# Experts of 96 slots in column tiles, with raw f32 weights, in place of 128 slots with split weights

## The reference

```python
g_idx = jnp.argmax(g_logits, axis=-1)
e_top, e_idx = lax.top_k(e_logits, TOP_K)              # TOP_K = 2 of 4 in that group
gates = jnp.sum(jax.nn.one_hot(ids, N_EXPERTS, dtype=f32) * e_w[..., None], axis=-2)
for e in range(N_EXPERTS):                              # 16 experts
    y = (jax.nn.silu(h @ w_gate[e]) * (h @ w_up[e])) @ w_down[e]   # 1024 -> 256 -> 1024
    out = out + gates[..., e:e + 1] * y.astype(f32)
```

## Time and profile before

| | |
|---|---|
| median of three runs | 513.7 us (513.49 to 515.2) |
| profiled execution, span from first to last instruction | 514.0 us |
| first gate/up product of the experts starts | 317.27 us |
| last down product ends | 480.59 us |
| TensorE busy | 464.2 us, 90% of the span |
| TensorE weight loads | 380.7 us, 74% |
| VectorE busy | 361.1 us, 70% |
| ScalarE busy | 257.9 us, 50% |
| GpSimd (POOL) busy | 104.8 us, 20% |
| DMA | 93.17 MB, mean 181 GB/s |

### The profile page before, as it was taken

The page is one execution under the profiler, slowest core; times in us unless marked ns, Lnnn a source line. Parts: engine busy times, 40 slices in busy tenths (PEclk is TensorE's granted clock), DMA queues, the critical chain, the costliest instruction groups (busy, mean ns, idle before and its releaser), DMA issues.

```text
span 514.0 us, 7284 instructions
## 1 busy us (share of the span) xinstructions
PE 464.2 (90%) x2541; PEld 380.7 (74%) x2541; DVE 361.1 (70%) x682; ACT 257.9 (50%) x484; POOL 104.8 (20%) x167
## 2 busy tenths in 40 slices
PE   6999899999999999999999988899999999999300
PEld 6879799878897777777787778787787778688100
DVE  4877515585676455776653769899998998998176
ACT  6663720643266436342231154588578678685021
POOL 5248001010100000000010032021323133132244
PEclk9999999999999999999989968899999999999855
DMA  8804404004006610510101598999999999921294
GB/s 303 201 11 166 172 0 160 5 1 164 1 2 178 157 62 0 177 49 1 42 1 62 162 342 311 421 383 405 357 344 396 379 365 376 355 92 46 80 341 179
DMA packets 32958, 93.17 MB, mean 181 GB/s; under 512 B 10104, under 2 KB 13312, under 8 KB 26784
## 3 DMA queue, kind: packets, MB, share of 16 engines
q1 hardware_dynamic: 27728, 82.81, 44.7%
q0 software_dynamic: 5200, 9.97, 5.2%
HBM read 87.85 MB, written 13.89 MB: 198 GB/s over the span
## 4 chain that ended last, share of the span: by engine, by line
PE 69%; DVE 15%; DMA 6%; ACT 4%; issue 3%; POOL 1%; SPq 1%; POOLq 0%; DVEq 0%; ACTq 0%
PE ps L1786 8%; PE ps L1788 7%; PE ps L1787 7%; PE ps L2140 4%; PE ps L2142 4%; PE ps L2141 4%; DVE gu_lo L1636 4%; PE ps L1998 3%; PE ps L1999 3%; PE ps L2000 3%; DMA xg<-h_rows,now_tok 2%; DMA pair<-y_pairs 2%; PE ps L2120 2%; PE ps L2023 2%; PE ps L2114 1%
## 5 line engine op out<-in xcount | busy, mean ns | idle before, releaser
L1636 DVE TENSOR_TENSOR gu_lo<-we_gu,gu_hi 128x1024 fp32r<-128x1024 f32 x64 | 74.4, 1220 | 0.8
L1016 ACT ACTIVATE gu_hi<-we_gu 128x1024 fp32r<-128x1024 f32 x64 | 63.3, 1057 | 0.0
L2140 PE MATMUL ps<-gu_hi,xT_hi 128*128 128x512 f32 x128 | 52.8, 412 | 3.3 <-DVE xT_lo L1630 3.2
L2142 PE MATMUL ps<-gu_hi,xT_lo 128*128 128x512 f32 x128 | 50.9, 398 | 0.0
L2141 PE MATMUL ps<-gu_lo,xT_hi 128*128 128x512 f32 x128 | 50.5, 394 | 0.0
L1786 PE MATMUL ps<-hT_hi,w_hi 128*128 128x288 f32 x160 | 48.6, 304 | 1.6 <-DVE w_lo_q L1129 0.8
L1786 PE MATMUL ps<-w_hi,hT_hi 128*128 128x512 f32 x96 | 38.9, 405 | 0.0
L1787 PE MATMUL ps<-w_lo,hT_hi 128*128 128x512 f32 x96 | 37.5, 390 | 0.0
L1786 PEld LDWEIGHTS ps<-hT_hi,w_hi 128*128 128x128 f32 x160 | 30.1, 188 | 5.0 <-issue 2.6
L2140 PEld LDWEIGHTS ps<-gu_hi,xT_hi 128*128 128x128 f32 x128 | 24.6, 192 | 9.6 <-issue 2.5
L826 ACT ACTIVATE w_hi<-ring,g_col 128x512 fp32r<-128x512 f32 (+1 forms) x48 | 28.8, 679 | 0.3 <-DMA ring<-in_w_in 0.3
(11 more groups left out here) (404 smaller groups left out, 1220.7 us busy)
## 6 DMA issues: line engine op xcount, KB each, us to landing
we_gu<-in_w_gate SPq DMA_DIRECT2D x16, 1024.0 KB, 8.3
we_gu<-in_w_up SPq DMA_DIRECT2D x16, 1024.0 KB, 12.9
we_d<-in_w_down SPq DMA_DIRECT2D x16, 1024.0 KB, 12.3
ring<-in_w_in SPq DMA_DIRECT2D x4, 2048.0 KB, 7.7
pair<-y_pairs SPq DMA_DIRECT2D x8, 512.0 KB, 7.8
ring<-in_w_in SPq DMA_DIRECT2D x3, 1024.0 KB, 8.3
x_first<-in_x_p SPq DMA_DIRECT2D x4, 512.0 KB, 9.9
x<-in_x_p SPq DMA_DIRECT2D x4, 512.0 KB, 3.9
```

The lines of the kernel that those rows point to most:

```text
L1016: act.activation(gu_hi[slot % 2][:, :, 2 * q:2 * q + 2, :], we_gu[slot][:, :, 2 * q:2 * q + 2, :], ACT.Copy).then_inc(gu_hi_done, 1)
L1636: dve.tensor_tensor(gu_lo[slot][:, :, 2 * q:2 * q + 2, :], we_gu[slot][:, :, 2 * q:2 * q + 2, :], gu_hi[slot % 2][:, :, 2 * q:2 * q + 2, : ...
L2140: pe.matmul(bank(0), xT_hi[:, c, :], gu_h[:, :, c, :], start=c == 0, stop=False)
L2142: last = pe.matmul(bank(0), xT_lo[:, c, :], gu_h[:, :, c, :], start=False, stop=c == KC - 1)
```

## The change

An expert gets 96 slots (`CAP`). Four experts fill 384 columns, which are three blocks of 128 (`PER`). The columns of a block are cut into column tiles of one width, each of one expert: block 0 is 96 columns of expert 0 and 32 of expert 1 (four tiles of 32), block 1 has 64 of expert 1 and 64 of expert 2 (two tiles of 64), block 2 has 32 of expert 2 and 96 of expert 3 (four tiles of 32). All products of the experts are plain f32 on raw weights; the splits and their buffers are gone.

```diff
+CAP = 96
+QUAD = 32
+PER = UNROLL * CAP // P
+MAX_OVER = (PAIRS - NE) // CAP
+AHEAD = 3
+def runs_of(b):
+    out = []
+    for q in range(P // QUAD):
+        u = (P * b + QUAD * q) // CAP
+        if out and out[-1][2] == u:
+            out[-1][1] += QUAD
+        else:
+            out.append([QUAD * q, QUAD, u])
+    return out
+def tiles_of(b):
+    runs = runs_of(b)
+    width = QUAD if any(n % (2 * QUAD) for _, n, _ in runs) else 2 * QUAD
+    return [(at + d, width, u) for at, n, u in runs for d in range(0, n, width)]
+PIECES = [(0, 0, 0, 96, 0), (0, 1, 0, 32, 96),
+          (1, 1, 32, 32, 0), (1, 1, 64, 32, 32), (1, 2, 0, 64, 64),
+          (2, 2, 64, 32, 0), (2, 3, 0, 32, 32), (2, 3, 32, 32, 64), (2, 3, 64, 32, 96)]
...
 # TensorE
-                    gu_h, gu_l = gu_hi[slot % 2], gu_lo[slot]
                     for c in range(KC):
-                        pe.matmul(bank(0), xT_hi[:, c, :], gu_h[:, :, c, :], start=c == 0, stop=False)
-                        pe.matmul(bank(0), xT_hi[:, c, :], gu_l[:, :, c, :], start=False, stop=False)
-                        last = pe.matmul(bank(0), xT_lo[:, c, :], gu_h[:, :, c, :], start=False, stop=c == KC - 1)
+                        for at_col, n, u in tiles_of(b):
+                            cols = slice(at_col, at_col + n)
+                            last = pe.matmul(ps[cols, 0, :], xT[:, c, cols], we_gu[u][:, :, c, :],
+                                             start=c == 0, stop=c == KC - 1)
                     last.then_inc(gu_ready, 1)
+                    pe.wait_ge(gathered[following], 16 * (i + (b + 1) // PER + 1))
+                    turn_half(following, 0, x_turned_a)
+                    turn_half(following, 1, x_turned_b)
+                    if b:
+                        down(i, b - 1)
+                    elif i is not first:
+                        down(i - 1, PER - 1)
+                    if i is first and b == PER - 1:
+                        over_slots()
                     pe.wait_ge(hh_ready, s + 1)
 # in down(i, b)
                 for half in range(2):
                     for f in range(2):
+                        for at_col, n, u in tiles_of(b):
+                            cols = slice(at_col, at_col + n)
+                            last = pe.matmul(ps[cols, 4 + 2 * (b % 2) + half, :], hhT[:, f, cols],
+                                             we_d[u][:, f, 512 * half:512 * half + 512], start=f == 0, stop=f == 1)
 # ScalarE and VectorE, per block, in this order
+                    act.activation(sg[:, :], ps[:, 0, 0:FE], ACT.Silu).then_inc(silu_ready, 1)
+                    take_x(s + 1)          # half of xT each
+                    take_y(i, b - 1)       # or (i - 1, PER - 1)
...
+                    dve.tensor_tensor(hh[:, :], sg[:, :], ps[:, 0, FE:2 * FE], ALU.mult).then_inc(hh_ready, 1)
+                    take_x(s + 1)
+                    take_y(i, b - 1)
+                    dve.tensor_copy(hhT[:, :, :], ps[:, 3, 0:2 * P].rearrange("p (c t) -> p c t", c=2)).then_inc(hhT_ready, 1)
 # VectorE, the table: nine pieces for each of the two tables
+            for b in range(PER):
+                fill(table_tok, 5, range(NE, 2 * NE), 0, b).then_inc(table_ready, 1)
 # SP
             expert(1, 1, 0, 2)
+            sp.wait_ge(out_ready, 2 * NT)
+            expert(2, 2, 0, 2)
             store_h2(NT - 1)
-            expert(0, 0, 2, 3)
-            expert(1, 1, 2, 3)
+            expert(3, 3, 0, 2)
...
             sp.wait_ge(gathered[0], 16)
+            for u in range(UNROLL):
+                expert(u, u, 2, 3)
+            with sp.Fori(1, TURNS) as i:
+                sp.wait_ge(gu_ready, PER * i - PER + 1)
+                expert(0, UNROLL * i, 0, 2)
+                sp.wait_ge(gu_ready, PER * i - PER + 2)
+                expert(1, UNROLL * i + 1, 0, 2)
+                sp.wait_ge(y_ready, PER * i - PER + 1)
+                expert(0, UNROLL * i, 2, 3)
+                sp.wait_ge(gu_ready, PER * i)
+                expert(2, UNROLL * i + 2, 0, 2)
+                expert(3, UNROLL * i + 3, 0, 2)
+                sp.wait_ge(y_ready, PER * i - PER + 2)
+                expert(1, UNROLL * i + 1, 2, 3)
+                sp.wait_ge(y_ready, PER * i)
+                expert(2, UNROLL * i + 2, 2, 3)
+                expert(3, UNROLL * i + 3, 2, 3)
 # POOL
-            for s in range(AHEAD):
+            for s in range(PER):
+                pool.wait_ge(table_ready, s + 1)
                 gather(s, table_tok[:, s:s + 1])
```

More of the change, by code:

```diff
@@ L601, in _ @@
                         e = sp.value_load(steer[0:1, bass.ds(UNROLL * i + slot + 1, 1)], min_val=0, max_val=NE - 1)
-                        expert(slot, e)
-            for par in range(2):
-                sp.wait_ge(stored[par], 8 * UNROLL * turns + 16)
+                        expert(slot, e, 0, 2)
+                        sp.wait_ge(y_ready, PER * i + PER * TURNS - (1 if slot < 2 else 0))
+                        expert(slot, e, 2, 3)
+            for b in range(PER):
+                sp.wait_ge(stored[b], 16 * more + 16 * TURNS + 16)
@@ L683, in _ @@
             pool.sem_inc(bias_ready, 1)
[L684 to L685 removed]
+            for out, n, first, step in ((iota16, NE, 0, 1), (iota8, OVER_UNITS, 0, 1),
+                                        (iota_p, P, 0, 1), (limits, TERMS, CAP, CAP)):
                 chain(pool.iota(out[:, :], pattern=[[step, n]], base=first, channel_multiplier=0,
@@ L746, in _ @@
                 gather(s, table_tok[:, s:s + 1])
-            pool.wait_ge(table_ready, 2)
+            pool.wait_ge(table_ready, PER + 1)
             pool.wait_ge(x_turned_b, 1)
[L749 to L760, removed]
@@ L784, in _, with scatter_later @@
-            with pool.Fori(1, turns) as i:
-                gather_next(i, 1)
-                for k in range(2, UNROLL + 1):
-                    gather_next(i, k)
-                    scatter_later(i, k - 2)
-                scatter_later(i, UNROLL - 1)
+                gather(b, now_tok[:, b, :])
+            def scatter_later(i, b):
+                s = PER * i + b - 2
+                was = (b - 2) % PER
+                pool.wait_ge(stored[was], 16 * i + (16 if b == 2 else 0))
+                pool.tensor_copy(now_pair[:, was, :], table[:, bass.ds(s, 1)]).then_inc(col_copied, 1)
+                pool.wait_ge(col_copied, 2 * PER * i - 2 * PER + 2 * b + 2)
+                pool.wait_ge(y_act, s + 1)
+                pool.wait_ge(y_dve, s + 1)
+                pool.sem_inc(dma_cleared, 1)
+                scatter(was, now_pair[:, was, :])
@@ new lines, in _ @@
+            with pool.Fori(1, more + TURNS) as i:
+                for b in range(PER):
+                    gather_next(i, b)
+                    scatter_later(i, b)
+            for b in range(PER - 2, PER):
+                s = PER * more + PER * TURNS - PER + b
+                pool.wait_ge(stored[b], 16 * more + 16 * TURNS)
+                pool.tensor_copy(now_pair[:, b, :], table[:, bass.ds(s, 1)]).then_inc(col_copied, 1)
+                pool.wait_ge(col_copied, 2 * PER * more + 2 * PER * TURNS - 2 * PER + b - PER + 3)
+                pool.wait_ge(y_act, s + 1)
+                pool.wait_ge(y_dve, s + 1)
+                pool.sem_inc(dma_cleared, 1)
+                scatter(b, now_pair[:, b, :])
@@ L1087, in _ @@
+            with act.Fori(1, more + TURNS) as i:
                 group_of_blocks(i)
+            take_y(more + TURNS - 1, PER - 1)
             for t in range(NT):
@@ L1697, in group_of_blocks @@
-                take_y(i, UNROLL - 1)
-            def down_low(i, slot):
-                for f in range(2):
-                    dve.wait_ge(d_hi_done, 2 * SHORT * i + 2 * slot + f + 1)
-                    dve.tensor_tensor(we_d_lo[slot][:, f, :], we_d[slot][:, f, :], we_d_hi[:, f, :].bitcast(F32),
-                                      ALU.subtract).then_inc(d_lo_done, 1)
+                    take_x(s + 1)
+                    if i is first and b == 0:
+                        weights()
+                    if b:
+                        take_y(i, b - 1)
+                    elif i is not first:
+                        take_y(i - 1, PER - 1)
```

391 lines of the change are left out of this document (135 added, 256 removed).

## The result

The changed kernel takes 506.24 us (median of four runs, 506.04 to 507.54), the kernel before beside it 513.6. The ratio is 0.9855, with a 95% interval of 0.9827 to 0.9884: 7.4 us faster. The forecast was 496.5, 17.2 us faster. The direction was right, and so was the mechanism of the steady blocks; the step at the start (the first chain of products at full pace) failed, and the size with it. Ratios are of fast executions alone, so that one execution of the kernel before, of 1592.6 us beside e5 to e8, does not count.

The account below looks back on a forecast made before the run. TensorE was taken to bound the kernel. First product at 318.3, first chain, ten blocks of 11.86 us, waits and tail put the last product at 463.4; 33.4 more gave span 496.8, time 496.5 us, range 489 to 503.

Parts of the forecast that it names:

- the mechanism of the steady blocks: Expert blocks on TensorE: tiles run beside each other, three blocks taking 35.6 us against 39.6 to 40.2 before.
- the first chain of products at full pace: First block's gate/up products on TensorE: eight steps at 0.86 us, 6.88 us.
- the changes of shape: Borders between column tiles and full-width work on TensorE: 0.5 us a block, bounds 0 and 1.0.
- the way from span to time: Final conversion: predicted span 496.8 us, measured median 0.3 us below the profiled span, so 496.5.
- A step of four tiles costs one plain product: Gate/up steps on TensorE: all tiles run beside each other, 0.86 us a step; bounds up to 3.44.
- A block, 11.86 us: Steady block on TensorE: gate/up 6.88, down 3.44, other work 1.04, shape changes 0.5 us.
- Weights hide: Expert weight loads: some 9 us in hand holds the whole lag, counted as nothing; other bound 8.4 us.
- The case of DMA in the lead: Rival: weight transfers set the pace, three groups at 38.4 us, +8.4 us, 505; chance 0.09.
- The start: Ahead of the experts: gather 2.5 us slower, first product moves from 317.27 to 318.3, between 316.4 and 321.
- The case of a falling clock: Rival: a long stretch of plain products could be granted 1.2 GHz, time above 620 us; chance 0.03.
- The end: After the last gate/up: 9.5 us to the end of the last product, then an unchanged 33.4 us.

Follow-up runs that it names:

- e5: Changed kernel with gate/up requests of experts 2 and 3 both behind the last store of h2; 508.33 us, ratio 0.9836.
- e8: Changed kernel with gate/up products issued tile by tile in place of step by step; 651.88 us in a single execution.
- e1: Changed kernel with one full-width tile per step, so part of the result is not computed; 500.81 us, ratio 0.9753.
- e6: Changed kernel with all tiles 32 wide, hh transposed next to x, hhT in three buffers and copied ahead of y; 503.29 us, ratio 0.9753.
- e11: e6 plus last h2 store ahead of expert 2's request, expert 3's gate/up request after the first gather, 36 idle products for 30; 498.66 us, ratio 0.969.
- e4: Changed kernel with expert 3's gate and up requested after the first gather landed, in place of before it; 504.81 us, ratio 0.9812.
- e9: Changed kernel with last h2 store ahead of expert 2's request, expert 3's gate/up request after the first gather, 36 idle products; 500.59 us, ratio 0.9755.
- e3: Changed kernel with 42 idle TensorE products ahead of the first gather, in place of 30; 503.27 us, ratio 0.9782.
- e10: The changed kernel itself run once more, on the same chip as e9 and e11; 505.86 us, ratio 0.9843.

## Why the prediction was wrong in size

The step that failed is the first chain at full pace. Two terms beside it were mis-sized: the changes of shape, and the way from span to time.

- *A step of four tiles costs one plain product.* Right: 7.01 us for eight, against 6.88, and the 0.13 is the border behind the chain. The Trainium skill, "TensorE: Matmul & The Clock Gate", section on packing small matmuls, offered a few ns per tile or a speedup of 2.38 for three; in these chains the first holds (12 passes in 1.49 us), the second doesn't show.
- *A block, 11.86 us.* Measured 12.10. The mis-sized term is the changes of shape. I had put 0.5 us on top of 1.04 for the rest; e1 measures the rest and the products at 11.41 (predicted 11.36) and the four borders at 0.69. Over the ten blocks from the second gate/up chain to the last it adds up to 2.3 us. The Trainium skill's "TensorEngine Tiling (Array Packing)", key properties of the tiling modes, says that a change of mode drains TensorE; e1 and e6 price the change at 0.13 to 0.21 us here.
- *Weights hide.* Right, and closer than I said: no weights are waited for at 12.1 us a block, 1.55 us at 11.4 (e1), 0.6 at 12.0 in e11, which starts its first product 4 us earlier. The case of DMA in the lead, which had 0.09, begins just beyond this kernel.
- *The start.* The first product came at 319.12, within the given bounds, but by luck. The gather landed at 316.8 as forecast (309.99 + 4.4 + 2.5), for another reason: it did not fly half as long again (5.0 us in place of 4.4) but was issued 1.9 us late. The store that should have landed by 308 or 309 landed at about 311. The sum had the queue ahead of it clear at 306, taking the full rate from the first request on; in e4 it runs dry at 309.1. There the engines moved 274 GB/s up to 295 and 420 after that, some 7.8 MB by 309.1 in place of 7.1 (worked out from the rates). The 0.8 us that is missing lies in the transposes and the copy of x: from the first transpose to the first product it is 2.26 us, 0.5 less than before, where I had taken off about 1.5. Of that, 0.3 is the clock (1.99 us in e9).
- *The first chain.* This step failed outright, and it is the largest single term: 6.88 predicted, 9.69 measured. The sum put TensorE's pause ahead of it at nothing. I had moved the gather without asking what TensorE does meanwhile: its idle products end at 314.8, it stands still for 2.0 us, and the chain then begins at a granted clock of 0.50 (1.2 GHz) and has the full clock only from about 324 on. The runs with a shorter pause (e3, e9) show 7.07 in its place. The case of a falling clock was among the rivals only for long plain chains, where it did not come.
- *The end.* 9.9 us from the last gate/up product to the last down product (predicted 9.5), and 34.4 from the last copy to the end, against 33.4. That 1 us is not of the change: on the path the load of the pairs takes 13.0 us here, 11.6 in the kernel before and 11.8 in e10, which is the same kernel as this one.
- *Span and time.* I took the median (513.7) and the profiled span (514.0) as measures of the same execution. In all later runs a span is 1.7 to 2.5 us below its own time, mostly 1.7 to 1.9, and the kernel before has spans of 511.3 to 513.5 in most executions. The profiled one was among its longest. So the last step, from span to time, needed 1.8 us more, not 0.3 less. The part ahead of the experts was no reason for the long span: the table's first write starts at 308.86 in the profile before and at 308.58 in the one after. The lower clock in its second block (e3) is some 1.6 us of it (eight products, 0.2 us each); whether its other executions have that too is not known.

The sum: 0.8 (start) + 2.8 (from the first chain to the second: 2.6 of clock, 0.2 of changes of shape) + 2.3 (the blocks to the last chain) + 0.5 (from there to the last product) + 1.1 (behind it) = 7.6 us in the span but for rounding, and 2.1 outside: 9.7, which is 506.2 - 496.5.

## What to carry to other kernels

In these plain f32 chains, column tiles of several small matrices run at the price of one product if neighbours in the instruction order lie on different tiles; each change of shape costs 0.13 to 0.21 us, so put what needs the same shape together. Before requesting a transfer earlier, look at what small store or gather comes behind it in the queue, and at who stands still until that lands: here a store of 256 KB came 2 us late behind 2 MB of weights, its consumer waited, and the chain behind that wait began at half the clock (2.6 us). Set a forecast against spans and times of the same execution, and ask whether the profiled execution is a typical one.

## What the runs showed of the hardware

- Four column tiles of 32 in plain f32, each streaming its own expert's weights, run together without a measurable loss (7.01 us against 6.86 for eight full-width products; down, with no border behind it, has 3.45 against 3.44).
- Issued tile by tile, four tiles of 32 take 22.5 us in place of 7.0 (e8); about two products of the next tile start early, 1.7 us at each border.
- After 2.0 us without products, the first chain ran 2.6 us longer (granted clock 0.50 in its first part); after 0.7 to 0.8 us (e9, e3) and after 1.7 us (e1) it did not.
- A gather of 128 rows took 4.4 us with few transfers beside it and 9.0 us with 4.2 MB of weights in flight on another queue.
